# Fourier and neighbourhood-attention block on one core: block differences moved to VectorE, first softmax inside the last value tile, w_fo pieces from the fifth step, weights split four steps after their load

## What is computed

```python
hx = modulate(rms_norm(x, norm1_g[l]), sh1, sc1)
fx, qx, kx, vx = split_projection(hx @ w_in[l])
qx = axial_rope(rms_norm(qx, q_norm_g[l]))
kx = axial_rope(rms_norm(kx, k_norm_g[l]))
y_four = fourier_mix(fx)
y_attn = neighbourhood_attention(qx, kx, vx, kc, vc, rpb[l])
gates = jax.nn.sigmoid(hx @ w_gate)
g_f, g_a = jnp.split(gates, 2, axis=-1)
merged = g_f * (y_four @ w_fo) + g_a * (y_attn @ w_ao)
x = x + g1 * (merged @ w_o)
...
x = x + g2 * ((jax.nn.relu(hx2 @ w_mlp1[l]) ** 2) @ w_mlp2[l])
```

## Time and profile before

| | |
|---|---|
| median of 3 runs | 2599.37 us (2597.89 to 2601.55) |
| profiled execution | 2600.51 us |
| its span in the profile | 2598.7 us |
| PE busy | 2541.8 us, 98% of the span |
| DVE, ACT, POOL busy | 1817.6, 1219.3, 226.4 us |
| mean granted clock of PE | 0.993 of full speed |
| HBM read, written | 316.89 MB, 91.23 MB |

### The profile page before, as it was taken

How to read it: one execution, slowest core, us unless ns; L and a number is a source line. 1 busy time by engine, 2 the same in 40 slices (tenths; PEclk the granted TensorE clock), 3 DMA queues, 4 the chain that set the end, 5 groups by cost and what they waited for, 6 DMA issues and landing times.

```text
span 2598.7 us, 41970 instructions
## 1 busy us (share of the span) xinstructions
PE 2541.8 (98%) x16772; PEld 2141.3 (82%) x16772; DVE 1817.6 (70%) x2564; ACT 1219.3 (47%) x1926; POOL 226.4 (9%) x254
## 2 busy tenths in 40 slices
...
GB/s 158 74 51 82 66 34 42 90 107 212 251 244 253 284 375 322 340 228 57 141 92 114 127 73 56 58 49 53 193 157 128 150 154 143 156 333 274 241 223 137
DMA packets 292610, 410.86 MB, mean 158 GB/s; under 512 B 16192, under 2 KB 163136, under 8 KB 292160
## 3 DMA queue, kind: packets, MB, share of 16 engines
...
HBM read 316.89 MB, written 91.23 MB: 157 GB/s over the span
## 4 chain that ended last, share of the span: by engine, by line
PE 74%; DVE 5%; ACT 2%; DMA 2%; issue 1%; SPq 0%; DVEq 0%; ACTq 0%
PE ps L1061 22%; PE ps L994 7%; PE ps L992 7%; PE ps L996 7%; PE ps L664 2%; PE ps L648 2%; PE ps L651 2%; PE ps L1193 2%; PE ps L1194 2%; PE ps L1195 2%; PE ps L778 2%; PE ps L774 2%; PE ps L776 2%; PE ps L1076 1%; PE ps L1255 1%; PE ps L1234 1%
## 5 line engine op out<-in xcount | busy, mean ns | idle before, releaser
L992 PE MATMUL ps<-Bh,Ah 128*128 128x512 f32 x896 | 349.6, 390 | 1.4 <-ACT vb L1876 1.4
L994 PE MATMUL ps<-Bh,Al 128*128 128x512 f32 x896 | 348.8, 389 | 1.5 <-DVE Al L2540 1.5
L996 PE MATMUL ps<-Bl,Ah 128*128 128x512 f32 x640 | 249.0, 389 | 0.0
L1898 ACT ACTIVATE ftr_h<-ftr_r 128x1024 fp32r<-128x1024 f32 x112 | 118.6, 1059 | 236.1 <-DMA ftr_r<-b_scratch 236.0
L2303 DVE TENSOR_TENSOR Wlo<-Wraw,Whi 128x1024 fp32r<-128x1024 f32 x84 | 102.8, 1241 | 156.2 <-ACT Whi L1678 155.8
L774 PE MATMUL ps<-Whi,Hh 128*128 128x256 f32 x736 | 211.9, 288 | 0.0
L1061 PE MATMUL ps<-ftr_h,wgt_h 128*128 128x512 f32 x848 | 210.1, 390 | 0.0
L1061 PE MATMUL ps<-ftr_l,wgt_h 128*128 128x512 f32 x848 | 209.4, 389 | 0.0
L1061 PE MATMUL ps<-ftr_h,wgt_l 128*128 128x512 f32 x848 | 209.4, 389 | 0.0
L776 PE MATMUL ps<-Wlo,Hh 128*128 128x256 f32 x736 | 208.1, 283 | 0.0
L778 PE MATMUL ps<-Whi,Hl 128*128 128x256 f32 x736 | 208.0, 283 | 0.0
...
## 6 DMA issues: line engine op xcount, KB each, us to landing
b_scratch<-qb SPq DMA_DIRECT2D x224, 256.0 KB, 3.0
...
pair<-in_m_w SPq DMA_DIRECT2D x128, 256.0 KB, 3.3
...
```

Source lines behind the costliest of these rows:

```text
L992: e.matmul(o, h[:, k, :], Bh[x][:, k, :], start=first and k == 0, stop=False, skip_group_check=not first)
L994: e.matmul(o, l[:, k, :], Bh[x][:, k, :], start=False, stop=False, skip_group_check=not first)
L996: i = e.matmul(o, h[:, k, :], Bl[x][:, k, :], start=False, stop=k == 3, skip_group_check=not first)
L1898: e.activation(ftr_h[p][:], ftr_r[p][:], ACT.Copy).then_inc(*S("a_hi").tick(2 * G))
```

## The change

Four things are reordered; no arithmetic of the reference is left out.

1. **Block differences on DVE in order of need.** `Tr[5]` (three DVE passes from `Hh` and `Hl` in place of four POOL instructions from `HT`) and the first sum of `Tr[4]` move to DVE; POOL keeps `Tlow`. ACT takes `t_hi(5)`, `t_hi(6)` and `t_hi(7)` later, DVE's `Tr[7]` passes come behind three weight sums, `gate_copy` of product 1 no longer waits for the transfer of `Yr` to its scratch.
2. **First softmax inside the last value tile.** `qk(0)` stands behind the fourth of 16 groups of the last value tile's second half, ACT takes `soft(0, 0)` and `soft(0, 1)` ahead of that tile's copy; the loop begins with step 1. The four rows of `Yb` are split one per step, in steps 1 to 4.
3. **w_fo pieces from the fifth step on.** `fo_piece(p)` stands in step p + 4 (`FO` is 4) in place of p + 1, so pieces 28 to 31 come after the loop; `fo_copy`, `fo_out` follow, the last of them after `o_out(31)`.
4. **Weights split four steps after their load.** SP loads at steps 8, 16, 24 as before; ACT and DVE split them in steps 12, 20, 28. Two weights formerly split in the last value tile go to steps 6 and 7, and the raw load of w_ao's tile that stood at step 32 goes behind the first round of gate loads.

```diff
                 for which in ("q", "k", "v"):
-                    if half == 0 and which != "v":
-                        q = 7 if which == "k" else 6
-                        pe.wait_ge(S("gate_copy").at(GSTEP[4, q]), S("gc_sum").at(4 * q + 3))
                     g = tm(nm(which), H2)
                     for s in range(2):
-                        for _ in range(16):
+                        if (half, which) == (0, "q"):
+                            pe.wait_ge(S("gate_copy").at(GSTEP[4, 6 + s]), S("gc_sum").at(4 * (6 + s) + 3))
+                        for n in range(16):
                             next(g)
+                            if (half, which, s, n) == (1, "v", 1, 3):
+                                qk(0)
                         if late:
...
                         late = (which, s) if which != "v" else None
-            for i in range(NP):
+            for i in range(1, NP):
                 qk(i)
-                if i:
-                    tr(i - 1, 0)
-                    fo_piece(i - 1)
-                    tr(i - 1, 1)
+                tr(i - 1, 0)
+                if i >= FO:
+                    fo_piece(i - FO)
+                tr(i - 1, 1)
                 if i > 1:
                     pv(i - 2)
-            fo_piece(NP - 1)
             rings["all"][1] = 3
...

+            fo_piece(NP - 4)
+            fo_piece(NP - 3)
             tr(NP - 1, 0)
+            fo_piece(NP - 2)
             pv(NP - 2)
-            ao_high(0, (0, 1))
             tr(NP - 1, 1)
-            ao_high(0, (2,))
-            ao_low(0, (0, 1))
+            fo_piece(NP - 1)
+            ao_high(0, (0, 1, 2))
             pv(NP - 1)
-            ao_low(0, (2,))
             ao_high(1, (0, 1, 2))
+            ao_low(0, (0, 1, 2))
             ao_high(0, (3,))
-            ao_low(0, (3,))
             ao_low(1, (0, 1, 2))
             ao_high(1, (3,))
+            ao_low(0, (3,))
             ao_low(1, (3,))
...
                     load_bias(pair, bm, "bm", biasM)
-                if i % 2 == 0:
-                    fo_out(i // 2 - 1)
-                    if i % 8 == 0:
-                        feed(upto(("w_fo", i // 4 - 2)))
-
+                if i % 2 and i > FO:
+                    fo_out((i - FO) // 2)
+                if i in (8, 16, 24):
+                    feed(upto(("w_fo", i // 4 - 2)))
+            fo_out(14)
+            fo_out(15)

...
                              ACT.Copy).then_inc(*freed(name))
-            t_hi(6)
+            t_hi(5)
             u_copy(1)
...
             u_post(1)
+            t_hi(6)

...
                     return
-                act.wait_ge(gproduct_full(s), S("y_out").at(0))
+                act.wait_ge(gproduct_full(s))
+                if x in (6, 7):
+                    act.wait_ge(S("y_out").at(0))
                 if x == 4:
...
             chan_out(0, 1)
-            t_hi(7)
             chan_out(1, 1)
-            for n in range(NG + 1):
-                if n:
-                    gate_copy(n - 1)
+            ga_part(3)
+            t_hi(7)
+            for n in range(1, NG + 1):
+                gate_copy(n - 1)
                 if n + 3 < NG:
...

+            def weights_between(i):
+                if i in (6, 7):
+                    feed(upto(((1, "v"), 1)) - 7 + i)
+                elif i % 8 == 4 and i > 4:
+                    feed(upto(("w_fo", (i - 12) // 4)))
+
             def y_hi(k):
...
                         name = ((half, which), s)
+                        if (half, which, s) == (1, "v", 1):
+                            table(LOG)
+                            soft(0, 0)
+                            soft(0, 1)
                         act.wait_ge(full_at(name))
...

-            table(LOG)
-            for i in range(NP):
+            for i in range(1, NP):
                 if i > 2:
                     o_out(i - 3)
-                if i:
-                    turned(i - 1, 0)
+                turned(i - 1, 0)
                 soft(i, 0)
-                if i:
-                    turned(i - 1, 1)
+                turned(i - 1, 1)
                 soft(i, 1)
-                if i == 0:
-                    for k in range(4):
-                        fy_hi(k)
-                elif i % 2 == 0:
-                    fo_copy(i // 2 - 1)
-                if i and i % 8 == 0:
-                    feed(upto(("w_fo", i // 4 - 2)))
+                if i <= 4:
+                    fy_hi(i - 1)
+                elif i % 2:
+                    fo_copy((i - FO) // 2)
+                weights_between(i)
             o_out(NP - 3)
             y_hi(0)
-            y_hi(1)
-            fo_copy(15)
             turned(NP - 1, 0)
+            fo_copy(14)
+            y_hi(1)
             o_out(NP - 2)
-            y_hi(2)
             turned(NP - 1, 1)
+            y_hi(2)
             o_out(NP - 1)
+            fo_copy(15)
             y_hi(3)
...

-            def t_part(n, to, a, b, how):
-                e.tensor_tensor(to, a, b, how).then_inc(*S("t_raw").tick((n + 1, 0)))
-                dve.wait_ge(S("t_raw").at((n + 1, 0)))
+            def t_sum(x, part, to, a, b, how):
+                n = (5, 6, 7, 4).index(x)
+                if part:
+                    dve.wait_ge(S("t_raw").at((n, int(part == 9 and x in (4, 5)))))
+                elif x == 6:
+                    dve.wait_ge(S("t_raw").at((0, 9)))
+                e.tensor_tensor(to, a, b, how).then_inc(*S("t_raw").tick((n, part)))

...
                 e.tensor_tensor(CD[a][1], cdr[:, a, :], CD[a][0].bitcast(F), ALU.subtract).then_inc(*S("cd_lo").tick(a))
+            dve.wait_ge(full_at(("ctx_k1", 0)), full_at(("ctx_k1", "T")), H2.lo_at(7))
+            t_sum(5, 0, Tr[5][:], block(Hh, 0, 1), block(Hh, 0, 0), ALU.subtract)
+            t_sum(5, 1, Tr[6][:], block(Hl, 0, 1), block(Hl, 0, 0), ALU.subtract)
+            t_sum(5, 9, Tr[5][:], Tr[5][:], Tr[6][:], ALU.add)
             feed(upto(("u0", 1)))
             u_lows(0)
-            t_lo(5)
-            dve.wait_ge(full_at(("ctx_k1", "T")), H2.lo_at(7))
-            t_part(0, Tr[6][:], block(Hh, 4, 1), Tr[5][:], ALU.subtract)
-            e.tensor_tensor(Tr[6][:], Tr[6][:], block(Hl, 4, 1), ALU.add).then_inc(*S("t_raw").tick((1, 1)))
+            t_sum(6, 0, Tr[6][:], block(Hh, 4, 1), Tr[5][:], ALU.subtract)
+            t_sum(6, 9, Tr[6][:], Tr[6][:], block(Hl, 4, 1), ALU.add)
             u_sums(1)
...
             u_lows(1)
+            t_lo(5)
             t_lo(6)
...
             ga_part(0)
-            dve.wait_ge(S("t_pool").at((1, 0)))
-            t_part(1, Tr[7][:], block(Hh, 4, 1), block(Hh, 0, 1), ALU.subtract)
-            e.tensor_tensor(Tr[7][:], Tr[7][:], Tlow[:], ALU.add).then_inc(*S("t_raw").tick((2, 1)))
-            ga_part(1)
             ga_sum(2)
+            ga_part(1)
             ga_part(2)
-            t_lo(7)
+            dve.wait_ge(S("t_low").at(0))
+            t_sum(7, 0, Tr[7][:], block(Hh, 4, 1), block(Hh, 0, 1), ALU.subtract)
+            t_sum(7, 9, Tr[7][:], Tr[7][:], Tlow[:], ALU.add)
             for n in range(NG + 1):
...
                     ga_part(n + 3)
-                if n == 2:
-                    dve.wait_ge(S("t_pool").at((2, 0)))
-                    t_part(2, Tr[4][:], Tr[4][:], Th[6][:].bitcast(F), ALU.subtract)
+                if n == 0:
+                    t_lo(7)
+                elif n == 1:
+                    dve.wait_ge(full_at(("chan", 0, 1)))
+                    t_sum(4, 0, Tr[4][:], block(Hh, 4, 0), Th[6][:].bitcast(F), ALU.subtract)
+                elif n == 2:
+                    t_sum(4, 1, Tr[4][:], Tr[4][:], Tl[6][:].bitcast(F), ALU.subtract)
                 elif n == 3:
-                    e.tensor_tensor(Tr[4][:], Tr[4][:], Tl[6][:].bitcast(F), ALU.subtract).then_inc(*S("t_raw").tick((3, 1)))
+                    t_sum(4, 9, Tr[4][:], Tr[4][:], block(Hl, 4, 0), ALU.add)
                 elif n == 4:
...
             pool.wait_ge(full_at(("dft", 1, 1)), H2.lo_at(7))
-            e.tensor_tensor(Tlow[:], block(Hl, 4, 1), block(Hl, 0, 1), ALU.subtract).then_inc(*S("t_pool").tick((1, 0)))
-            pool.wait_ge(full_at(("chan", 0, 1)))
-            e.tensor_tensor(Tr[4][:], block(Hh, 4, 0), block(Hl, 4, 0), ALU.add).then_inc(*S("t_pool").tick((2, 0)))
+            e.tensor_tensor(Tlow[:], block(Hl, 4, 1), block(Hl, 0, 1), ALU.subtract).then_inc(*S("t_low").tick(0))

```

More of the change, by code:

```diff
@@ L243, in build @@
         Tl = {x: at(f"Tl{x}", [P, 4, 512], R, o) for x, o in ((5, S_(0)), (6, S_(4)), (7, R1A + 16384), (4, S_(8)))}
-        Tr = {x: at(f"Tr{x}", [P, 4, 512], F, o) for x, o in ((5, S_(10)), (6, S_(4)), (7, R1A + 16384), (4, S_(8)))}
+        Tr = {x: at(f"Tr{x}", [P, 4, 512], F, o) for x, o in ((5, S_(0)), (6, S_(4)), (7, R1A + 16384), (4, S_(8)))}
         Tlow = at("Tlow", [P, 4, 512], F, R1A + 24576)
@@ L411, in build @@
         GOUT = {2: (0, 0, 0), 7: (1, 1, 1), 4: (2, 1, 0), 3: (3, 0, 1)}
+        FO = 4
         def gring(s):
@@ L1199, in tensor_program @@
```

(29 more changed lines are left out.)

21 lines of the change are left out of this document (6 added, 15 removed).

## The result

The changed kernel takes 2584.26 us (median of 4 runs, 2583.07 to 2586.5) against 2600.01 before: a ratio of 0.994, interval 0.9926 to 0.9953. That is 15.7 us faster; 30.2 were forecast, and the range ended at 2584.0. The profiled execution took 2583.07 us, with a span of 2581.2, 17.5 less than before.

The account below looks back on a forecast made before the run. PE, busy for 98% of the span, was taken as the bound, so only its idle time and slow clock could go. 18.0 + 4.5 + 17 - 9.3 = 30.2 us gained, about 2569.5 us against the median; range 2557 to 2584.

Parts of the forecast that it names:

- Block differences: u0: Ahead of u0: `HT` without POOL beside it ends earlier, gaining 3.6 us of waiting and 1.5 of half clock.
- Transform and gates: Channel transform to gates: waits of 1.2, 1.5, 9.1 us go, clock returns 2.3; `Tl[4]` about 1.2 late.
- rival D: At u1 or the transform: DVE's added passes come late, PE waits; total gain 23, 2576.5 us; chance 0.08.
- First softmax: Start of attention, up to `qk(6)`: gain 4.5 us, bounds 0 and 8; steps 2 to 5 take 7.0 each.
- Weights four steps later: Attention steps 9, 17, 25: 18.9 us loss goes, five splits cost 2.0; net gain 17, bounds 13 and 19.
- Rival B: Attention: DVE becomes the bound, steps take 6.5 us; gain 19, about 2581, or 2585 with the tail's bound; chance 0.15.
- w_fo pieces later: After the attention loop: three pieces 4.2, copy waits 0.7 and 1.6, merge 2.8; 9.3 us lost, bounds 5 and 13.
- Rival F: Attention: many short waits keep the clock at 1.2 GHz, making the kernel slower, 2605 us; chance 0.04.
- three signs of being wrong: Attention steps near 7 us to the end, attention clock below 0.95, or w_o product wait of 8 us or more.

Follow-up runs that it names:

- e4: Kernel before the change, with only the split of the weights loaded in steps 8, 16, 24 moved to steps 12, 20, 28: 2584.54 us, ratio 0.9941.
- e1: Changed kernel with SP's `fo_out` one step later, behind that step's mask load: 2576.19 us, ratio 0.9905.
- e2: Changed kernel with DVE's attention step waiting only for the mask table it reads, SP's order unchanged: 2574.06 us, ratio 0.99.
- e3: Changed kernel with ACT's `fo_copy(15)` right behind `turned(31, 1)`, ahead of `y_hi(2)` and `o_out(31)`: 2580.5 us, ratio 0.9926.

## Why the prediction was wrong

- **Block differences: u0.** Forecast 3.6 + 1.5; measured 4.42 - 0.48 = 3.9 of waiting, and full clock. Right. The first half of the rule weighed there (the Trainium skill, "Perfetto Trace Analysis", Optimizing Scalar/DVE Operations), that a saturated DVE may hand work on to GpSimd, did not hold ahead of u0: `HT` alone took 5.38 for 9.51. Its second half, that GpSimd and DVE share a read port, agrees with this; the trace shows the slowdown and not the port.
- **Transform and gates.** 1.5, 9.1 and 2.3 went as forecast, the wait for `Tl` at product 4 came at 1.1 for 1.2. The 1.2 us at the start of the transform went too, though `Th[5]`'s sum was not "long done": ACT waited 3.7 us for it. But a new wait of 2.1 came 6 us into the transform, for `Wlo`. That is rival D at a third of its price. The sentence that failed is "they fit with 2.6 to spare, if the idle time lies where they need it": 2.4 us of DVE's idle time lay ahead of the passes, where `Tr[5]` waited for the transposes of the context's key tile. And only two of the transform's four low parts come "right behind" the new passes; the third stood behind `Tr[6]` as well. The stretch as a whole missed by 1 us, or 1.7 without the 0.8 that was not the change's.
- **First softmax.** 4.5 forecast, 4.6 measured, though not quite as drawn: steps 1 to 5 take 5.3, 10.5, 6.3, 7.6 and 7.5 us where I had 8.9 in step 1, for `Yb`, and then steps of 7.0. The long step is one later, and the sum came out.
- **Weights four steps later.** This is the step that failed: "Net 17; bounds 13 and 19", against 5.1. The late split itself did what I said: e4 takes 19.1 us out of the three long steps, for the 18.9 forecast (16.0 alone, after its three splits). The five splits were under-priced: 0.4 each, where steps 13, 21 and 29 paid 1.0, and steps 7 and 8 paid 0.4 and 1.5, 5 us in all for 2.0; I had counted DVE's 1.15 us and neither the idle time for ACT's high part ahead of it nor that the next step's maxima queue behind both. The larger part, 9.5 us by e1, was no term at all. I moved `fo_out` with the pieces and did not look at what it is queued ahead of on SP: the mask load, of which the trace of before showed one wait of 0.9 us, so no slack. With 9.5 and 3 more in the sum it would have been 17.7, as the span shows 17.5.
- **Rival B** named DVE as the new bound, 2581 to 2585, which the time fits; its mechanism does not, but for the 5 us of the steps that carry a split. The steps that carry none keep their length (10 to 12: 5.8, 5.8 and 5.9 in both kernels). From `qk(6)` to `pv(29)` DVE is busy for 139 of 176 us in 26 steps, 1.4 idle in each (the window below, columns as in the earlier trace rows), and e1 and e2 change nothing in DVE's work and give 8 to 10 us back. A time that agrees is no proof of the cause.

```profile
1640.50:1816.30 175.80, 164.57 (x1488) 132.08 (x1488) 139.31 (x399) 113.78 (x336) 0.00 (x0) 0.98 0.16 50
```

- **w_fo pieces later.** 9.3 forecast, 9.3 measured, and its parts much as drawn: waits of 0.5 and 1.5 for `fo_copy` (0.7 and 1.6 forecast) and 2.4 in the product with w_o (2.8). That leaves 4.9 for the three pieces, priced at 4.2, so the exact agreement is luck. e3 shows the last wait to be the copy's place; that w_ao's raw tile costs 1.3 us there is not shown.
- **Rival F** did not come: the clock was 0.98 in the same window. None of the prediction's three signs of being wrong showed either (steps of 7 us to the end, a clock below 0.95, a wait of 8 us in the product with w_o): they were signs for terms that it had, not for one that it lacked.
